# The start of a two-block transformer layer: relative-position masks as signs on ScalarE, the first pass's low parts all on VectorE

## The chip, the cores and the metric

The kernel runs on one core of one Trainium2 chip. The metric is the device time of one execution in microseconds (us), the median of three runs. Engines: TensorE (PE), VectorE (DVE), ScalarE (ACT), GpSimd (POOL) and SyncE (SP), which issues all DMAs here.

## The reference

One sequence of 256 tokens of width 2048 goes through two blocks. Only the head of the first one matters here:

```
mod = silu(c) @ ada_w + ada_b                  # six vectors of 2048: shift, scale, gate, twice
h   = rms_norm(x) * (1 + sc_a) + sh_a
proj = h @ w_in                                # 2048 x 3968 here, latents, rope keys and differential q, k, v
bias = rel_bias[t5_bucket(key_pos - query_pos)]   # 256 x 256 for each of 8 heads
s1, s2 = q1 @ k1 * scale + bias, q2 @ k2 * scale + bias
a = softmax(s1) - lam * softmax(s2)
lam = exp(sum(lq1*lk1)) - exp(sum(lq2*lk2)) + lambda_init
```

Everything is float32. Behind this come the attention of both kinds, an output projection, a convolved gated feed-forward, and a second block with windowed, selected and compressed attention. The change leaves all of that alone.

## The kernel before

**Products.** A float32 product is made as three of a rounded type: each weight half (128 x 1024, 512 KB) is loaded into one of 8 slots of `raw`; ScalarE copies it rounded into `w_hi` (`hi`, L863 to L870), and the difference `raw - w_hi` goes to `w_lo` (`lo`, L1179 on VectorE or L1693 on GpSimd). Both have 4 slots. `product` (L509) issues three matmuls of 128x128 by 128x256 for a weight tile: L514, L515, L516. `hi(h)` waits until TensorE has done with half h - 4. Which engine makes a low part is fixed by the set `POOL_HALVES` (L126): in the first pass the odd halves are GpSimd's, in the second every other one too.

**The passes.** The input projection runs in two passes of 31 units (output tiles), each over 8 of the 16 tiles of the model's width; one unit is one weight half, 24 matmuls. The first pass (`U_IN`) needs the modulation of tiles 0 to 7 of x, the second (`U_IN_B`) of tiles 8 to 15.

**The modulation vectors.** `ada_w` comes in 192 loads of 512 KB, called ada here. VectorE scales each by an element of `silu(c)` and adds it up in `ada_acc` (`ada`, L1187 to L1200). The first 32, ada 0 to 31, make shift and scale of the width's first half, the next 32 those of the second. TensorE then sums over partitions (`mod_sum`, L538 to L547: 16 matmuls of one column for a pair of vectors, f32), VectorE adds the bias (`mod_out`, L1202), and `modulate` (L1230) makes h with ScalarE's `h_high` (L892): x times scale and 1/rms, rounded, and the low part, tile by tile.

**The loads.** SP issues them in one fixed order (`load_order`, L163): ada 0 to 27, weights 0 and 1, ada 28 to 31, weights 2 and 3, then weights and ada 32 to 63 spread evenly. Load n waits until what lies in slot n - 8 is used: for an ada, VectorE's step; for a weight, its low part (`slot_free`, L475). The inputs stand ahead: positions, 0.6 MB of parameters, 0.9 MB of constants; the 2 MB of x stand behind the first eight loads. So load 36, weight 4, waits for the low part of weight 0.

**The bias.** t5_bucket is a step function of the distance. The kernel makes 64 masks of 128 x 256 in bf16, each telling whether key minus query has reached a bucket's start (partitions: 32 starts x 4 groups of keys; one mask for each of 64 key indices), and TensorE sums bucket differences over them, in three bf16 parts: 4 groups of 16 masks, 96 matmuls a group, 48 for each of two query tiles (L665 to L680, 384 in all). ScalarE evicts the eight banks (`bias_ready`, L994 to L1003, four copies each). The banks of the last two groups are shared: bank 6 with the square sums of x, bank 7 with the sums for lambda, so the order in which these stand is an order of banks.

The masks come about like this: ScalarE adds the key's position to `start` for eight masks at a time (`distances`, L970 to L977, 8 activations of 128x256 a block) into one of two buffers, GpSimd compares the block with zero (L1690) and frees the buffer. GpSimd makes blocks 0 to 4 and VectorE blocks 5, 6 and 7 by one comparison each (`last_masks`, L1360), between its first ada.

**Order on each engine up to the first pass.** ScalarE: distances 0 and 1, Sin for the rope tables, distances 2, the squares of x (`squares`, L883, 16 of them into 4 slots), distances 3 and 4, Exp for lambda, root of the mean square, a wait for all of GpSimd's masks, eight evictions, `hi(0)`, `hi(1)`, `h_high`, `hi(2)`, `hi(3)`. TensorE: sum for lambda (behind the product on VectorE at L1396), square sums (L552), bias groups 0, 3, 1, 2, `mod_sum(0)`, `mod_sum(1)`, units. VectorE: positions, bias differences (`delta`), ten steps on 128x256 for cosine and sine (L1379 to L1394), the lambda product, ada 0 to 31 with the masks, after ada 24 the mean of the squares and lambda (L1406 to L1409), after ada 28 the reciprocal; then `mod_out(0)`, `mod_out(1)`, `modulate`, the low parts of weights 0 and 2, and in turns low parts and ada (L1418 to L1422).

```python
            def slot_free(n):
                if n >= RAW_SLOTS:
                    what, i = LOADS[n - RAW_SLOTS]
                    if what == "w":
                        sp.wait_ge(*lo_done(i))
                    else:
                        sp.wait_ge(ada_used, i + 1)
```

## Time and profile before

| | before |
|---|---|
| median of 3 runs | 1955.62 us (1954.48 to 1956.82) |
| the profiled execution | 1954.82 us, of which its span is 1953.0 us |
| mean granted TensorE clock | 0.957 of full |
| PE busy | 1775.6 us, 91% of the span |
| DVE busy | 1253.0 us, 64% |
| ACT busy | 870.9 us, 45% |
| POOL busy | 274.2 us, 14% |
| HBM read | 372.85 MB |

The span runs from the first to the last instruction of the profiled execution; the rest of its time lies around it. Busy time is time in which an engine has an instruction in work; a share over the whole span mixes stages with different limits, so the rows below are taken by stage. Matmuls overlap each other by the time that one needs to drain, so a single one's duration (0.28 us at full clock) is longer than the step from one to the next. A row of the timeline merges equal neighbours: start, time from the first's start to the last's end, engine, line, operation, output and inputs, shapes, count, and in brackets the idle time before it with what ended it.

### The profile page before, as it was taken

The numbers are of one execution on the slowest core, as the hardware profiler recorded it, in microseconds if no ns is written. First come the engines' busy times: TensorE is split into PE (matmuls) and PEld (weight loads), VectorE is DVE, ScalarE is ACT, GpSimd is POOL, SyncE is SP. The second block draws the span as 40 slices with busy tenths as digits, with TensorE's granted clock in tenths as the row PEclk, the third lists the DMA queues.
The fourth block names the chain that finished last, engine by engine and source line by source line (L and its number), as shares of the span: only waits on it lengthen the run. The fifth ranks groups of instructions, "written<-read, shape, count | busy, mean of one in ns | idle before, by whom it ended". The sixth has DMA issues, their size and how long they took to land.

```text
span 1953.0 us, 33440 instructions
## 1 busy us (share of the span) xinstructions
PE 1775.6 (91%) x13960; PEld 1706.7 (87%) x13960; DVE 1253.0 (64%) x1749; ACT 870.9 (45%) x1424; POOL 274.2 (14%) x131
## 2 busy tenths in 40 slices
PE   1399997879998999999999999999699999988997
PEld 1399996778987999999999999999599999866797
DVE  8669698655567766767757756655644446556544
ACT  4444434453445544534535445434444443465442
POOL 7544341001441000000000000000200000152000
PEclk9699998998988999999999999999899999998999
DMA  8499677633973666656656655544155544431041
GB/s 303 162 373 375 229 273 262 202 117 135 337 286 116 224 206 211 232 193 219 230 184 227 223 188 184 184 163 161 54 173 184 183 177 160 162 108 65 33 173 55
DMA packets 102822, 377.13 MB, mean 193 GB/s; under 512 B 11536, under 2 KB 11664, under 8 KB 102544
## 3 DMA queue, kind: packets, MB, share of 16 engines
...
q8 instruction: 111, 1.82, 0.4%
q14 instruction: 39, 0.32, 0.0%
HBM read 372.85 MB, written 2.10 MB: 192 GB/s over the span
## 4 chain that ended last, share of the span: by engine, by line
issue 45%; PE 36%; DVE 13%; POOL 3%; ACT 2%; DMA 1%; SPq 0%; ACTq 0%; DVEq 0%; POOLq 0%
PE ps L514 9%; PE ps L515 9%; PE ps L516 9%; DVE ada_acc L1199 4%; POOL masks L1690 2%; DVE probs L1310 1%; PE ps L596 1%; DVE stats L1284 1%; PE ps L545 1%; DVE w_lo L1184 1%; POOL probs L1684 1%; PE ps L552 1%; PE ps L630 1%; PE ps L615 1%; ACT w_hi L869 1%
## 5 line engine op out<-in xcount | busy, mean ns | idle before, releaser
L514 PE MATMUL ps<-h_hi,w_hi 128*128 128x256 f32 x3264 | 944.0, 289 | 28.2 <-DVE h_lo L1251 8.4
L515 PE MATMUL ps<-h_lo,w_hi 128*128 128x256 f32 x3264 | 930.7, 285 | 0.0
L516 PE MATMUL ps<-h_hi,w_lo 128*128 128x256 f32 x3264 | 930.2, 285 | 0.0
L1184 DVE TENSOR_TENSOR w_lo<-raw,w_hi 128x1024 fp32r<-128x1024 f32 x448 | 552.0, 1233 | 387.7 <-ACT w_hi L869 385.7
L869 ACT ACTIVATE w_hi<-raw 128x1024 fp32r<-128x1024 f32 x512 | 538.8, 1057 | 428.8 <-PE ps L516 408.7
L514 PEld LDWEIGHTS ps<-h_hi,w_hi 128*128 128x128 f32 x3264 | 633.0, 194 | 34.9 <-issue 14.1
L515 PEld LDWEIGHTS ps<-h_lo,w_hi 128*128 128x128 f32 x3264 | 633.9, 194 | 1.1
L516 PEld LDWEIGHTS ps<-h_hi,w_lo 128*128 128x128 f32 x3264 | 633.6, 194 | 0.0
L1199 DVE SCALAR_TENSOR_TENSOR ada_acc<-raw,c_act,ada_acc 128x1024 f32<-128x1024 f32 x180 | 257.7, 1461 | 0.4 <-DMA raw<-in_ada 0.3
L1696 POOL TENSOR_TENSOR w_lo<-raw,w_hi 128x1024 fp32r<-128x1024 f32 x64 | 172.0, 2695 | 426.9 <-ACT w_hi L869 426.9
L514 PE MATMUL ps<-g_hi,w_hi 128*128 128x256 f32 x704 | 200.2, 284 | 3.7 <-DVE g_lo L1528 3.7
L515 PE MATMUL ps<-g_lo,w_hi 128*128 128x256 f32 x704 | 199.8, 284 | 0.0
L516 PE MATMUL ps<-g_hi,w_lo 128*128 128x256 f32 x704 | 199.5, 283 | 0.0
L1684 POOL TENSOR_TENSOR probs<-y,rstd 128x256 f32<-128x256 f32 x32 | 25.1, 803 | 814.5 <-DVE rstd L1228 809.5
L514 PEld LDWEIGHTS ps<-g_hi,w_hi 128*128 128x128 f32 x704 | 134.6, 191 | 4.2 <-DVE g_lo L1528 3.9
L516 PEld LDWEIGHTS ps<-g_hi,w_lo 128*128 128x128 f32 x704 | 132.9, 189 | 0.0
L515 PEld LDWEIGHTS ps<-g_lo,w_hi 128*128 128x128 f32 x704 | 132.5, 188 | 0.3
L1074 ACT ACTIVATE conv<-ps,params 128x256 f32<-128x256 f32 x88 | 49.8, 566 | 152.1 <-PE ps L516 152.1
L1520 DVE SCALAR_TENSOR_TENSOR conv<-ps,params,conv 128x255 f32<-128x255 f32 x88 | 42.5, 482 | 94.3 <-ACT conv L1074 94.3
L917 ACT ACTIVATE probs<-ps,stats 128x128 f32<-128x128 f32 (+1 forms) x112 | 48.7, 439 | 108.0 <-DVE stats L1288 76.5
L874 ACT ACTIVATE proj<-ps 128x256 f32<-128x256 f32 x79 | 30.6, 387 | 130.1 <-PE ps L516 130.1
L552 PE MATMUL ps<-probsT,mean_mat 128*128 128x256 f32 x204 | 62.6, 428 | 16.9 <-ACT probsT L881 16.6
...
## 6 DMA issues: line engine op xcount, KB each, us to landing
raw<-in_weights SPq DMA_DIRECT2D x512, 512.0 KB, 3.6
raw<-in_ada SPq DMA_DIRECT2D x192, 512.0 KB, 4.9
...
```

The lines of the kernel that those rows point to most:

```text
L514: nc.tensor.matmul(out, wh, hi[:, k, :], start=start, stop=False)
L515: nc.tensor.matmul(out, wh, lo[:, k, :], start=False, stop=False)
L516: last = nc.tensor.matmul(out, wl, hi[:, k, :], start=False, stop=stop)
L552: nc.tensor.matmul(ps[:, OUT + NORM[stage] % 2, 0:S], mean_mat[:, :], squares_in(slot), start=first, stop=last).then_inc(sq_used, 1)
L869: nc.scalar.activation(w_hi[:, h % W_SLOTS, :], raw[:, raw_slot("w", h), :], ACT.Copy).then_inc(hi_split, 1)
L917: last = nc.scalar.activation(probs[:, s, off:off + w], ps[:, SCORE + i % 2, off:off + w], ACT.Exp, bias=stats[:, s, 2 + qt:3 + qt], scale ...
L1074: nc.scalar.activation(conv[:, j, :], ps[:, BANK[u], 0:S], ACT.Identity, bias=params[:, col + b:col + b + 1], scale=params[:, col + w1:col ...
L1184: V.tensor_tensor(w_lo[:, h % W_SLOTS, :], raw[:, raw_slot("w", h), :], w_hi[:, h % W_SLOTS, :].bitcast(F32), ALU.subtract).then_inc(lo_dv ...
L1199: V.scalar_tensor_tensor(out=out, in0=part, scalar=c_act[:, k:k + 1], in1=out, op0=ALU.mult, op1=ALU.add).then_inc(ada_used, 1)
L1520: V.scalar_tensor_tensor(out=conv[:, j, 1:S], in0=ps[:, BANK[u], 0:S - 1], scalar=params[:, w0:w0 + 1], in1=conv[:, j, 1:S], op0=ALU.mult, ...
L1684: nc.gpsimd.tensor_tensor(probs[:, at % 2, 0:S], src(k), rstd[:, n % 2, :], ALU.mult).then_inc(scaled, 1)
L1696: nc.gpsimd.tensor_tensor(w_lo[:, h % W_SLOTS, :], raw[:, raw_slot("w", h), :], w_hi[:, h % W_SLOTS, :].bitcast(F32), ALU.subtract).then_i ...
```

## The change

The masks become signs: ScalarE makes all 64 in one activation each, `Sign(start + key position)`, straight into `masks`, four groups of 16 (`signs`). The starts are shifted by a half, so that no distance gives zero; with -1 and 1 in place of 0 and 1 the differences are halved and the last bucket's value is added for the constant part (`tab_last`, two more small steps on VectorE). Distances, their buffers, `neg_pos_k`, GpSimd's and VectorE's comparisons and their semaphores go. TensorE takes the groups in the order 0, 1, 2, 3, the sums for lambda ahead of them and Exp's wait ahead of group 3; the square sums of x come behind all groups, once six evictions are done. ScalarE: signs, Sin, Exp, six evictions, squares, two evictions, root, `hi(0)`, `hi(1)`. The low parts of the first pass are all VectorE's, those of weights 0 and 1 right behind ada 31 and ahead of `mod_out(0)`, those of 2 and 3 behind `modulate`. GpSimd does nothing between its first memsets and the low parts of the second pass. The diff's core:

```diff
-POOL_HALVES = set(range(1, N_IN, 2)) | set(range(N_IN + 1, 2 * N_IN, 2)) | set(range(H_O, H_FF, 2)) | set(
+POOL_HALVES = set(range(N_IN + 1, 2 * N_IN, 2)) | set(range(H_O, H_FF, 2)) | set(
     range(H_CMP + 2, H_OUT2 + 4))
...
-        BIAS_GROUPS = [0, 3, 1, 2]
-        POOL_MASKS = 5
...
             nc.tensor.matmul(ps[:, OUT + 1, 0:2], mean_mat[0:64, :], lam[0:64, 0:2], start=True,
                              stop=True).then_inc(lam_sum, 1)
-            mean_square("x0", KT)
-
-            pe.wait_ge(bias_delta, 1)
-            pe.wait_ge(lam_exp, 1)
-            pe.wait_ge(mean_ready, 1)
-            for i in BIAS_GROUPS:
-                if i == 3:
-                    pe.wait_ge(last_mask, 2)
-                elif i == 2:
-                    pe.wait_ge(last_mask, 3)
-                    pe.wait_ge(bias_mask, POOL_MASKS)
-                else:
-                    pe.wait_ge(bias_mask, 2 * i + 2)
-                for qt in range(0, 2):
+
+            def bias_sums(i):
+
+                pe.wait_ge(bias_mask, i + 1)
+                for qt in range(2):
                     for k in range(16):
                         for part in range(3):
-                            last = nc.tensor.matmul(
-                                ps[:, ds(4 * qt + i, 1), 32 * k:32 * k + 32].rearrange("p a n -> p (a n)"),
-                                masks[:, 16 * i + k, ds(P * qt, P)],
-                                delta3[:, part, :], start=part == 0, stop=part == 2)
+                            last = nc.tensor.matmul(ps[:, 4 * qt + i, 32 * k:32 * k + 32],
+                                                    masks[:, 16 * i + k, P * qt:P * qt + P], delta3[:, part, :],
+                                                    start=part == 0, stop=part == 2)
                     last.then_inc(bias_summed, 1)
+
+            pe.wait_ge(bias_delta, 1)
+            for i in range(3):
+                bias_sums(i)
+            pe.wait_ge(lam_exp, 1)
+            bias_sums(3)
+            pe.wait_ge(bias_ready, 6)
+            mean_square("x0", KT)
             pe.wait_ge(bias_ready, 8)
             mod_sum(0)
...
-            def distances(b):
-
-                if b >= 2:
-                    act.wait_ge(bias_mask, b - 1)
-                for k in range(8):
-                    last = nc.scalar.activation(distance[b % 2][:, k, :], start, ACT.Identity,
-                                                bias=pos_k[:, 8 * b + k:8 * b + k + 1])
-                last.then_inc(distance_ready, 1)
-
-            act.wait_ge(start_ready, 1)
-            distances(0)
-            distances(1)
-
-            act.wait_ge(angle_ready, 1)
-            nc.scalar.activation(cs1[:, :, :], cs1[:, :, :], ACT.Sin).then_inc(cs_ready, 1)
-            distances(2)
-            act.wait_ge(inputs_loaded[4], 16)
-            squares("x0", KT, lambda k: x[:, k, :])
-            distances(3)
-            distances(4)
-            act.wait_ge(lam_sum, 1)
-            nc.scalar.activation(lam[:, 2:4], ps[:, OUT + 1, 0:2], ACT.Exp).then_inc(lam_exp, 1)
-            root("x0")
-            act.wait_ge(bias_mask, POOL_MASKS)
-            for n in range(8):
+            def signs(i):
+
+                for k in range(16 * i, 16 * i + 16):
+                    last = nc.scalar.activation(masks[:, k, :], start, ACT.Sign, bias=pos_k[:, k:k + 1])
+                last.then_inc(bias_mask, 1)
+
+            def bias_out(n):
+
                 act.wait_ge(bias_summed, n + 1)
-                b = 4 * (n % 2) + BIAS_GROUPS[n // 2]
+                b = 4 * (n % 2) + n // 2
                 kk = 16 * (b % 4)
                 for grp in range(4):
                     last = nc.scalar.activation(
@@ -1001,6 +977,21 @@
                         ps[:, b, :].rearrange("p (k g h) -> p k g h", g=4, h=HEADS)[:, :, grp, :],
                         ACT.Copy, scale=1.0 / DIFF_SCALE)
                 last.then_inc(bias_ready, 1)
+
+            act.wait_ge(start_ready, 1)
+            for i in range(4):
+                signs(i)
+            act.wait_ge(angle_ready, 1)
+            nc.scalar.activation(cs1[:, :, :], cs1[:, :, :], ACT.Sin).then_inc(cs_ready, 1)
+            act.wait_ge(lam_sum, 1)
+            nc.scalar.activation(lam[:, 2:4], ps[:, OUT + 1, 0:2], ACT.Exp).then_inc(lam_exp, 1)
+            for n in range(6):
+                bias_out(n)
+            act.wait_ge(inputs_loaded[4], 16)
+            squares("x0", KT, lambda k: x[:, k, :])
+            for n in (6, 7):
+                bias_out(n)
+            root("x0")
             hi(0)
...
-            chain.link(V.tensor_scalar(neg_pos_k[:, :], pos_k[:, :], -1.0, None, ALU.mult))
             dve.wait_ge(inputs_loaded[3], 16)
 
             V.tensor_scalar(start, pos, con("start"), -1.0, ALU.add, ALU.mult).then_inc(start_ready, 1)
-
-            def last_masks(b):
-                dve.wait_ge(start_ready, 1)
-                V.tensor_tensor(masks[:, 8 * b:8 * b + 8, :], start.unsqueeze(1).broadcast_to([P, 8, S]),
-                                neg_pos_k[:, 8 * b:8 * b + 8].unsqueeze(2).broadcast_to([P, 8, S]), ALU.is_ge
-                                ).then_inc(last_mask, 1)
 
             dve.wait_ge(inputs_loaded[0], 16)
             dve.wait_ge(zeros_ready, 2)
             chain.link(V.scalar_tensor_tensor(out=delta[:, 0, :], in0=par("tab_prev"), scalar=con("prev_sign"),
                                               in1=par("tab_next"), op0=ALU.mult, op1=ALU.add))
+            chain.link(V.tensor_tensor(delta[:, 0, :], delta[:, 0, :], par("tab_last"), ALU.add))
+            chain.link(V.tensor_scalar(delta[:, 0, :], delta[:, 0, :], 0.5, None, ALU.mult))
...
             for i in range(32):
                 ada(i)
-                if i in (1, 2, 4):
-                    last_masks({1: 6, 2: 7, 4: 5}[i])
-                elif i == 24:
+                if i == 24:
                     mean("x0", KT, D)
                     dve.wait_ge(lam_exp, 1)
                     chain.link(V.tensor_tensor(lam[:, 4:5], lam[:, 3:4], lam[:, 2:3], ALU.subtract))
                     chain.link(V.tensor_scalar(lam[:, 4:5], lam[:, 4:5], -LAMBDA_INIT, None, ALU.add))
                 elif i == 28:
                     invert("x0")
+            lo(H_IN)
+            lo(H_IN + 1)
             mod_out(0)
             mod_out(1)
             modulate("x0", lambda k: scale_cols[:, 0, k:k + 1], SH_A, 0, SLAB)
-            lo(H_IN)
             lo(H_IN + 2)
+            lo(H_IN + 3)
             item = 32
             for j in range(4, N_IN + 2):
                 lo(H_IN + j)
...
-            for b in range(POOL_MASKS):
-                pool.wait_ge(distance_ready, b + 1)
-                nc.gpsimd.tensor_scalar(masks[:, 8 * b:8 * b + 8, :], distance[b % 2], 0.0, None, ALU.is_ge
-                                        ).then_inc(bias_mask, 1)
-
             def lo(h):
 
                 pool.wait_ge(hi_split, h + 1)
                 nc.gpsimd.tensor_tensor(w_lo[:, h % W_SLOTS, :], raw[:, raw_slot("w", h), :],
                                         w_hi[:, h % W_SLOTS, :].bitcast(F32), ALU.subtract).then_inc(lo_pool, 1)
 
-            for h in range(H_IN + 1, H_IN_B, 2):
-                lo(h)
             for h in range(H_IN_B + 1, H_UQ, 2):
...
+    last = np.where(np.arange(P)[:, None] % 32 == 0, nxt[-1:], 0.0)
...
-    put("start", np.tile(starts, 4))
+    put("start", np.tile(starts - 0.5, 4))
```

## Rows read from the trace of the kernel before

**Rows 1.** Stretches of 20 us: busy time of each engine, clock, DMA share and rate.
```profile
core 0: us, PE busy (x) PEld busy (x) DVE busy (x) ACT busy (x) POOL busy (x), PEclk, DMA share, GB/s
...
40.00:60.00 20.00, 0.00 (x0) 0.00 (x0) 18.50 (x17) 0.00 (x0) 20.00 (x1) 0.51 1.00 390
...
100.00:120.00 20.00, 20.00 (x162) 20.00 (x161) 9.85 (x9) 8.13 (x13) 7.80 (x4) 0.95 1.00 391
```

**Rows 2.** Timeline of the start, ScalarE and GpSimd: masks, distances, tables, evictions.
```profile
8.20 6.47 ACT L975 ACTIVATE bias<-probs,pos_k 128x256 f32<-128x256 f32 x16
...
11.57 10.81 POOL L1690 TENSOR_SCALAR masks<-bias 128x2048 bf16<-128x2048 f32 x2 [7.91 <-ACT bias L975]
...
22.56 0.63 ACT L984 ACTIVATE cs<-cs 128x512 f32<-128x512 f32 x1 [7.89 <-DVE cs L1394]
...
26.46 48.66 POOL L1690 TENSOR_SCALAR masks<-bias 128x2048 bf16<-128x2048 f32 x3 [4.08 <-ACT bias L975]
...
63.42 3.30 ACT L975 ACTIVATE bias<-probs,pos_k 128x256 f32<-128x256 f32 x8 [25.91 <-POOL masks L1690]
66.74 1.28 ACT L991 ACT_TABLE_LOAD   x1
68.03 0.17 ACT L991 ACTIVATE lam<-ps 128x2 f32<-128x2 f32 x1
...
75.16 7.39 ACT L999 ACTIVATE bias<-ps 128x128 f32<-128x128 f32 x32 [5.22 <-POOL masks L1690]
```

**Rows 3.** Timeline of PE: bias sums, mod sums, first pass's first product, second unit, next mod sums.
```profile
68.30 9.93 PE L676 MATMUL ps<-delta,masks 128*128 128x32 bf16 x384 [32.71 <-ACT lam L991]
...
82.59 6.99 PE L545 MATMUL ps<-mean_mat,ada_acc 128*128 128x1 f32 x32 [4.37 <-ACT bias L999]
...
97.50 0.58 PE L514 MATMUL ps<-h_hi,w_hi 128*128 128x256 f32 x1 [7.92 <-DVE w_lo L1184]
...
102.38 0.28 PE L514 MATMUL ps<-h_hi,w_hi 128*128 128x256 f32 x1
...
188.77 3.69 PE L545 MATMUL ps<-mean_mat,ada_acc 128*128 128x1 f32 x32
```

**Rows 4.** Timeline of the squares of x on ScalarE and their sums on PE.
```profile
26.29 1.32 ACT L881 ACTIVATE probsT<-x 128x256 f32<-128x256 f32 x4
26.74 8.85 PE L552 MATMUL ps<-probsT,mean_mat 128*128 128x256 f32 x32 [3.46 <-ACT probsT L881]
...
30.45 3.87 ACT L881 ACTIVATE probsT<-x 128x256 f32<-128x256 f32 x9 [0.32 <-PE ps L552]
```

**Rows 5.** Timeline of VectorE at the start: cosine step, ada, mean, reciprocal, second mod_out.
```profile
11.37 4.66 DVE L1387 SCALAR_TENSOR_TENSOR cs<-cs 128x256 f32<-128x256 f32 x3
...
22.65 1.40 DVE L1196 TENSOR_SCALAR ada_acc<-raw,c_act 128x1024 f32<-128x1024 f32 x2
...
34.17 12.03 DVE L1199 SCALAR_TENSOR_TENSOR ada_acc<-raw,c_act,ada_acc 128x1024 f32<-128x1024 f32 x10
...
58.09 0.41 DVE L1222 TENSOR_SCALAR rstd<-ps 128x256 f32<-128x256 f32 x1
...
76.79 1.74 DVE L1228 RECIPROCAL rstd<-rstd 128x256 f32<-128x256 f32 x1
...
89.69 0.17 DVE L1206 TENSOR_TENSOR mod<-ps,params 128x8 f32<-128x8 f32 x1 [2.90 <-PE ps L545]
```

**Rows 6.** VectorE in the first pass: all ada of 140 to 190 us; one low part.
```profile
L1199 DVE SCALAR_TENSOR_TENSOR ada_acc<-raw,c_act,ada_acc 128x1024 f32<-128x1024 f32 x19 | 40.6, 2177 | 0.0
...
109.70 1.23 DVE L1184 TENSOR_TENSOR w_lo<-raw,w_hi 128x1024 fp32r<-128x1024 f32 x1 [3.14 <-ACT w_hi L869]
```

**Rows 7.** Timeline at the second pass's start: its second mod_out; its second unit's first product.
```profile
193.27 0.17 DVE L1206 TENSOR_TENSOR mod<-ps,params 128x8 f32<-128x8 f32 x1
...
201.07 0.28 PE L514 MATMUL ps<-h_hi,w_hi 128*128 128x256 f32 x1
```

**Rows 8.** Timeline of SP's queue: three weight loads, the last waiting for weight 0's low part.
```profile
74.50 23.30 SPq L488 DMA_DIRECT2D raw<-in_weights  x3
```

9 lines of the change are left out of this document (3 added, 6 removed).

## The prediction

> **What bounds the kernel now.** I read the busy share in stretches first. From 100 to 120 us the PE is busy for all 20 us, with the DMA engines full beside it; from 40 to 60 us it does nothing at all, at a granted clock of about half, while GpSimd is busy for all 20 us [rows 1]. So the kernel has a start during which TensorE waits, and a first pass during which it doesn't. The timeline of ScalarE and GpSimd shows what fills the start: GpSimd makes five mask blocks, two in 10.81 us and three in 48.66 us, the last ending at 75.1 us; ScalarE's distances wait 25.9 us for a buffer that GpSimd has not freed; eight evictions of the bias follow [rows 2]. Only then do the mod sums run (6.99 us), and with the modulation of x behind them the first matmul of the pass starts at 97.50 us and its second unit at 102.38 us [rows 3]. From there to the mod sums of the second half at 188.77 us lie 30 units of 24 products in 86.4 us: 2.88 us a unit, 0.12 us a product, which is PE's own step at the full clock, so nothing waits in it [rows 3]. The start is the target; the first pass must keep its pace.
>
> **The new start, along ScalarE.** Each term is a duration of the trace of before. The steps go along one path; VectorE's own start and the loads are held against it further down.
> 1. The signs. 64 activations of 128x256 take the place of 40 distances. Sixteen distances took 6.47 us, 0.404 us each [rows 2], so 64 x 0.404 = 25.9 us from the same start, 8.20: 34.1 us. No row shows Sign. Bounds from the nearest rows: Square from SBUF at the same width, 9 in 3.87 us or 0.43 us each [rows 4], makes it 1.7 us more; below, nothing excludes that a bf16 output is a tenth cheaper, 2.6 us less. I take 0.404, the row with the same input, width and per-partition bias.
> 2. Sin 0.63, one table load 1.28, Exp 0.17 [rows 2]: 36.2 us. The row of the load ends where Exp begins (66.74 + 1.28 against 68.03), so the load costs 1.28 us. The Trainium skill, in "ScalarE: Activation LUTs", section "What ACT_TABLE_LOAD costs", adds a drain of about 1.38 us to it; by that page this path would be 1.4 us longer and the time 1929.8 us instead of 1928.4. The rows show no such gap.
> 3. Bias sums of groups 0 to 2 cost nothing: 96 matmuls each, a quarter of 9.93 us [rows 3], run from 23 us at the latest (the first ada, at 22.65, stands right behind the lambda product that PE waits for [rows 5]), each behind its own 16 signs, the third from 27.6 us, all under the signs and the table load; uncovered they are 2.5 us each. Group 3 waits for Exp, since its bank holds the lambda sums, and ends at 38.7 under the evictions.
> 4. Six of eight evictions: 7.39 us for all 8 [rows 2], 0.92 each, 5.5 us: 41.8 us. This order is forced: the square sums use the bank of group 2's second half.
> 5. The squares. Before, from the first square at 26.29 to the end of their sums at 26.74 + 8.85 = 35.59 us: 9.3 us, the first ones at ScalarE's wait for a slow PE [rows 4]. Again PE comes from idleness, so the same: 51.1 us. Were it warm, 16 squares would take 16 x 0.43 = 6.9 us, 2.4 less. The load of x, issued behind eight loads, had landed by 26.3 us and is no term.
> 6. VectorE. The mean 0.41, two small operations for lambda (one of that size, the modulation's bias, took 0.17; I count 0.4 with their waits), ada 25 to 30 at 12.03 / 10 = 1.20, and the reciprocal 1.74 between them [rows 5]: 9.8 us, so the last ada that the first mod sum wants is done at 60.8 us. Root and evictions 6 and 7 on ScalarE (1.8 + 1.28 + 0.4 from 49.8) are under the four ada ahead of the reciprocal.
> 7. Mod sums 7.0 us, again from idleness [rows 3]: the second mod_out at 67.8 us. It was at 89.69 [rows 5]: 21.9 us earlier.
>
> **The low parts of weights 0 and 1 moved ahead of the modulation.** They take 2 x 1.23 us [rows 6] on VectorE, under the mod sums (ada 31 ends at 62.0, they at 64.5): nothing, and 2.5 us if the sums were warm. What they free is the first unit, which now follows h tile by tile as the second half's does: there 193.27 to 201.07 from the modulation's bias to the second unit [rows 7], 7.8 us, where before it was 102.38 - 89.69 = 12.7 us. 4.9 us more. The second unit then starts at 75.6 us: **26.8 us earlier**. Behind SP's queue the gain is larger still: it waited 23.3 us for slots of the first weights [rows 8], and everything behind is queued in order. Now the stream restarts at 63 us, 13 us ahead of the second unit, where it had 4.5.
>
> **VectorE's start.** Three masks go; two operations of about 0.2 us come into the chain of the bias differences, ahead of everything behind it, and one outside it goes. Its cosine steps beside GpSimd's masks took 4.66 us for three, where the mean over the same 128x256 took 0.41 [rows 5]; alone they would start ada some microseconds sooner. Even if they don't, ada 24 ends at 22.65 + 0.4 + 1.4 + 23 x 1.20 = 52.1 us [rows 5], 1.0 behind the squares. So this is worth 0 to 1 us on the path; I take 0, since the masks of GpSimd beside those steps are gone. The loads: 28 of 0.52 MB and 3.7 MB of inputs and x are 18.4 MB; at the 390 GB/s of the full stretch [rows 1] they have landed at 47 us or soon after, ahead of their use. The cover of all this is the 1.0 us and more by which ScalarE is late; without it, VectorE's 1.20 us an ada is the path.
>
> **The first pass.** All low parts are VectorE's: per unit 1.23 + 1.10 ada. Beside GpSimd an ada took 2.18 us on average; alone 1.20 [rows 5, 6]. 1.23 + 1.32 = 2.55 us, under PE's 2.88: hidden by PE, with 0.33 us a unit to spare. VectorE takes over 15 low parts. Each of them now waits on VectorE's queue for its high part, and the ada behind it with it, whose slot SP wants back; but a high part is ready at 1.5 us after the unit that frees its buffer, PE wants the low part 8.6 us after it (three units), and ada follow in the order in which SP loads them, so no low part waits for a load that lies behind its own. SP's waits on GpSimd's low parts become waits on VectorE's, at the same places. GpSimd's next work, the second pass's low parts, waits for its high parts as before. The second pass and all behind it keep their program and their pace: 0, and nothing there can swallow the gain, since the loads come as much sooner as PE does.
>
> **Sum.** The profiled execution took 1954.82 us, 1.82 us around its span of 1953.0 and 0.8 us under the median of 1955.62. 1954.82 - 26.8 = 1928.0 us; the median would by the same step be 1928.8, and I give the middle, 1928.4 us.
>
> **Rivals.**
> - **Forecast, 0.72:** 1928.4, its own range 1924 to 1932 (cold and warm PE in steps 5 and 7, at most 2.4 and 3.5 less; Sign at 0.43, 1.7 more).
> - **ScalarE's chain is longer, 0.15.** Sign may need another table set: one load ahead of it and one back for Sin, 2 x 1.28 us; and were Sign a quarter dearer than the distance, that would be 6.5 us. For it: ScalarE is the bound, each us counts. Against: Identity, Copy and Square needed no load in the rows. 1931 to 1937. The skill's same page, "Table sets: the hidden batching unit", names relu, copy, identity and abs as in every set, not Sign; no row here bears on Sign.
> - **VectorE bounds the first pass, slower, 0.03.** If the 2.18 us is not GpSimd's doing but the price of an operation with two inputs from SBUF beside full DMA, and the low parts come to share it, a unit costs 2.10 x 2.18 = 4.6 us, 1.7 over PE, 29 times: +49, net +22, 1977 us. Its turning point is 3.8 us a unit, or 1.81 an operation. For it: it is what VectorE's rows show in the pass. Against: ten ada at 1.20 us from 34 to 46 us [rows 5], and a low part in the pass at 1.23 [rows 6]. If ada alone keeps 2.18, 3.6 a unit, the gain is 26.8 - 21 = 6: 1949 us, 0.03. By the skill's "SBUF — State Buffer", section "Who interferes with whom", a VectorE operation with two SBUF inputs and a GpSimd one that reads exclude each other for a whole instruction, the later one waiting. The rows fit it (GpSimd's mask blocks, 5.4 us each in the first two, took 16.2 in the last three, beside ada at 1.20 [rows 2, 5]); by it neither case can come.
> - **Start hidden anyway, 0.02.** The masks never were the end, or the signs run no sooner than GpSimd's masks did: then the mod sums stay where they are and so does the time, 1955. ScalarE's waits of 25.9 and 5.22 us for GpSimd speak against it [rows 2].
> - **More than the sum, 0.05.** Warm PE throughout: 26.8 + 5.9, 1922.
>
> **Numbers.** A measurement of this kernel can tell about 0.2%, 4 us, from no change. Faster by more: 0.95, same 0.02, slower 0.03. The range of 1921 to 1937 takes in the first, the second and the last case: 0.92, of which I leave a tenth for their own tails.
>
> **What would show it.** Right: the signs end near 34 us; first-pass matmul near 70; second unit near 75.6 with 30 units of 2.88 behind; ada at 1.20 in the pass; SP's stream restarting near 63. Wrong: a table load ahead of Sign; PE waiting in the pass for VectorE's low parts or for weights; a mod sum that starts after 65 us. The forecast fails if VectorE is over 2.88 us a unit or ScalarE's chain to Exp is over 40 us.

## The result, and the profile after

The kernel with the change takes 1922.45 us (median, 1922.31 to 1923.67), the one before beside it 1955.57 us (1954.48 to 1956.82): a ratio of 0.9832, 95% interval 0.9815 to 0.9849, 33.1 us faster. The forecast was 1928.4 us, from a gain of 26.8. The profiled execution took 1922.31 us, its span is 1920.5 us, the mean granted clock 0.959 (0.957 before).

The page of the kernel after, the engines' busy time and the groups that the change touches (busy us, mean ns, then the idle time before):

```profile
PE 1774.3 (92%) x13960; PEld 1705.6 (89%) x13960; DVE 1235.6 (64%) x1762; ACT 879.3 (46%) x1448; POOL 175.7 (9%) x111
...
L1175 DVE TENSOR_TENSOR w_lo<-raw,w_hi 128x1024 fp32r<-128x1024 f32 x463 | 570.4, 1233 | 380.5 <-ACT w_hi L862 378.3
...
L1190 DVE SCALAR_TENSOR_TENSOR ada_acc<-raw,c_act,ada_acc 128x1024 f32<-128x1024 f32 x180 | 237.6, 1340 | 2.2 <-DMA raw<-in_ada 2.2
...
L1677 POOL TENSOR_TENSOR w_lo<-raw,w_hi 128x1024 fp32r<-128x1024 f32 x49 | 131.8, 2698 | 507.9 <-ACT w_hi L862 507.9
```

PE's busy time is the one of before within 1.3 us; what went is waiting. VectorE makes the odd low parts too and is busy for 17 us less, of which its three masks are 6.8; GpSimd is busy for 98 less.

The timeline of the kernel after, from its start to the second unit of the first pass (start, us, engine, line, what, and the wait ahead of it); it answers to [rows 2 to 5] and [rows 8]:

```profile
8.82 25.64 ACT L966 ACTIVATE masks<-probs,pos_k 128x256 bf16<-128x256 f32 x64
...
12.40 1.34 DVE L1373 SCALAR_TENSOR_TENSOR cs<-cs 128x256 f32<-128x256 f32 x3
...
14.98 1.40 DVE L1187 TENSOR_SCALAR ada_acc<-raw,c_act 128x1024 f32<-128x1024 f32 x2
...
34.36 0.61 ACT L985 ACTIVATE cs<-cs 128x512 f32<-128x512 f32 x1
34.99 1.28 ACT L987 ACT_TABLE_LOAD   x1
36.29 0.17 ACT L987 ACTIVATE lam<-ps 128x2 f32<-128x2 f32 x1
36.36 5.66 ACT L975 ACTIVATE bias<-ps 128x128 f32<-128x128 f32 x24
...
36.51 2.74 PE L662 MATMUL ps<-delta,masks 128*128 128x32 bf16 x96 [5.67 <-ACT lam L987]
...
42.37 8.66 PE L547 MATMUL ps<-probsT,mean_mat 128*128 128x256 f32 x32 [3.12 <-ACT probsT L874]
...
51.06 0.42 DVE L1213 TENSOR_SCALAR rstd<-ps 128x256 f32<-128x256 f32 x1 [3.63 <-PE ps L547]
...
51.78 4.87 DVE L1190 SCALAR_TENSOR_TENSOR ada_acc<-raw,c_act,ada_acc 128x1024 f32<-128x1024 f32 x4
...
56.57 1.74 DVE L1219 RECIPROCAL rstd<-rstd 128x256 f32<-128x256 f32 x1
...
60.76 6.96 PE L540 MATMUL ps<-mean_mat,ada_acc 128*128 128x1 f32 x32 [9.73 <-DVE ada_acc L1190]
61.73 2.35 DVE L1175 TENSOR_TENSOR w_lo<-raw,w_hi 128x1024 fp32r<-128x1024 f32 x2
64.11 0.33 SPq L483 DMA_DIRECT2D raw<-in_ada  x1
...
67.83 0.17 DVE L1197 TENSOR_TENSOR mod<-ps,params 128x8 f32<-128x8 f32 x1 [3.12 <-PE ps L540]
...
69.85 0.55 PE L509 MATMUL ps<-h_hi,w_hi 128*128 128x256 f32 x1 [2.13 <-DVE h_lo L1242]
...
75.80 0.41 PE L509 MATMUL ps<-h_hi,w_hi 128*128 128x256 f32 x1
```

The path reads from the top: 64 signs in one block with no table load ahead of them, Sin, one load, Exp, six evictions, squares and their sums, the mean, six more ada with the reciprocal between them, the mod sums, the second mod_out, h tile by tile. The waits in brackets tell which engine is late: VectorE stood for 3.63 us ahead of the mean, waiting for PE's square sums and so for ScalarE.

A stretch of the first pass after, as in [rows 1]:

```profile
100.00:120.00 20.00, 20.00 (x169) 20.00 (x169) 17.81 (x16) 9.15 (x15) 0.00 (x0) 1.00 0.99 380
```

And VectorE's groups in the first pass (mean ns behind the comma), after, and then before:

```profile
L1190 DVE SCALAR_TENSOR_TENSOR ada_acc<-raw,c_act,ada_acc 128x1024 f32<-128x1024 f32 x30 | 40.2, 1351 | 0.0
L1175 DVE TENSOR_TENSOR w_lo<-raw,w_hi 128x1024 fp32r<-128x1024 f32 x29 | 35.5, 1224 | 11.8 <-ACT w_hi L862 11.8
```

```profile
L1199 DVE SCALAR_TENSOR_TENSOR ada_acc<-raw,c_act,ada_acc 128x1024 f32<-128x1024 f32 x29 | 54.8, 1927 | 0.3 <-DMA raw<-in_ada 0.3
L1184 DVE TENSOR_TENSOR w_lo<-raw,w_hi 128x1024 fp32r<-128x1024 f32 x15 | 18.3, 1217 | 17.1 <-ACT w_hi L869 17.1
```

PE is busy throughout with GpSimd at 0.00. Twice as many low parts cost VectorE only 2.6 us on balance, since an ada came down from 1.93 to 1.35 us on average once GpSimd was quiet. These means hide that an ada has two durations. Of the 29 before, 20 took 1.27 to 1.28 us and nine 3.0 to 3.4, each of these beside a low part on GpSimd that had begun before it. Of the 30 after, 29 took 1.28 us. The last took 3.43, beside GpSimd's first low part of the second pass; it is among these three, with GpSimd's row below:

```profile
156.42 5.82 DVE L1190 SCALAR_TENSOR_TENSOR ada_acc<-raw,c_act,ada_acc 128x1024 f32<-128x1024 f32 x3
...
158.20 2.96 POOL L1677 TENSOR_TENSOR w_lo<-raw,w_hi 128x1024 fp32r<-128x1024 f32 x1 [154.53 <-ACT w_hi L862]
```

**Where the time went.** Six marks of each trace, in us from the start of its span. The mod sums are counted from zero: 0 and 1 stand ahead of the first pass, 2 at its end, 4 ahead of the output projection, 6 ahead of the feed-forward, 7 ahead of the feed-forward's last group. The runs below are in it too, so that each can be read against the others.

| kernel | mod sum 0 | second mod_out | first eviction of the pass | mod sum 2 | mod sum 4 | span |
|---|---|---|---|---|---|---|
| before | 82.59 | 89.69 | 102.58 | 188.77 | 458.91 | 1953.0 |
| after | 60.76 | 67.83 | 76.04 | 162.35 | 429.76 | 1920.5 |
| after_again | 61.26 | 68.32 | 76.10 | 161.85 | 427.36 | 1918.2 |
| e1_signs_only | 63.40 | 70.47 | 82.71 | 168.91 | 434.68 | 1925.9 |
| e2_lows_only | 83.05 | 90.14 | 98.04 | 184.24 | 451.22 | 1945.3 |
| e3_lows_late | 61.13 | 68.20 | 81.38 | 167.57 | 437.95 | 1928.8 |
| e4_more_signs | 68.58 | 75.64 | 83.43 | 169.20 | 438.80 | 1929.4 |
| e5_mean_late | 57.79 | 64.86 | 72.64 | 158.39 | 427.18 | 1918.0 |
| e6_pool_beside | 62.39 | 69.46 | 77.25 | 175.53 | 446.90 | 1937.7 |
| s1_before_shifted | 85.54 | 92.64 | 105.64 | 191.82 | 461.91 | 1955.9 |
| e7_order | 55.85 | 62.92 | 70.70 | 156.56 | 426.11 | 1916.9 |
| e8_order_warm | 56.32 | 61.49 | 69.66 | 155.84 | 426.35 | 1917.2 |
| p1_before_moved | 82.85 | 89.95 | 102.58 | 188.77 | 458.39 | 1949.3 |
| p2_best_h_moved | 55.66 | 61.81 | 69.69 | 154.29 | 422.28 | 1887.2 |

Of the 32.5 us between the spans, 26.5 were gained by the first eviction. The first pass gave 0.1 back (86.3 us from the first eviction to mod sum 2, 86.2 before). From there to mod sum 4 the kernel after is 2.7 us quicker (267.4 against 270.1 us), and behind mod sum 4 it is 3.4 us quicker (1490.7 against 1494.1). The change edits no instruction in either of these last two stretches. So two questions: are my reasons for the 26.5 the right ones, and where do the other six come from?

### The profile page after: what moved, and what is told of

Same layout as the page of the kernel before. It is cut to its first block, busy times and chain, and to the rows that moved or that the text cites. A ratio compares the mean times of both kernels' runs of the same rounds, so it can differ in the third digit from the quotient of the medians.

```text
span 1920.5 us, 33456 instructions
## 1 busy us (share of the span) xinstructions
PE 1774.3 (92%) x13960; PEld 1705.6 (89%) x13960; DVE 1235.6 (64%) x1762; ACT 879.3 (46%) x1448; POOL 175.7 (9%) x111
## 4 chain that ended last, share of the span: by engine, by line
issue 45%; PE 40%; DVE 10%; ACT 3%; POOL 1%; DMA 1%; SPq 0%; ACTq 0%; DVEq 0%; POOLq 0%
PE ps L509 11%; PE ps L510 11%; PE ps L511 11%; DVE ada_acc L1190 3%; DVE probs L1301 1%; PE ps L591 1%; ACT masks L966 1%; DVE stats L1275 1%; PE ps L547 1%; PE ps L540 1%; POOL probs L1670 1%; PE ps L625 1%; PE ps L610 1%; PE ps L574 1%; PE ps L633 1%
## 5 line engine op out<-in xcount | busy, mean ns | idle before, releaser
L1175 DVE TENSOR_TENSOR w_lo<-raw,w_hi 128x1024 fp32r<-128x1024 f32 x463 | 570.4, 1233 | 380.5 <-ACT w_hi L862 378.3
L1190 DVE SCALAR_TENSOR_TENSOR ada_acc<-raw,c_act,ada_acc 128x1024 f32<-128x1024 f32 x180 | 237.6, 1340 | 2.2 <-DMA raw<-in_ada 2.2
L1677 POOL TENSOR_TENSOR w_lo<-raw,w_hi 128x1024 fp32r<-128x1024 f32 x49 | 131.8, 2698 | 507.9 <-ACT w_hi L862 507.9
```

Of the source, the lines that this page charges most:

```text
L1175: V.tensor_tensor(w_lo[:, h % W_SLOTS, :], raw[:, raw_slot("w", h), :], w_hi[:, h % W_SLOTS, :].bitcast(F32), ALU.subtract).then_inc(lo_dv ...
L1190: V.scalar_tensor_tensor(out=out, in0=part, scalar=c_act[:, k:k + 1], in1=out, op0=ALU.mult, op1=ALU.add).then_inc(ada_used, 1)
L1677: nc.gpsimd.tensor_tensor(w_lo[:, h % W_SLOTS, :], raw[:, raw_slot("w", h), :], w_hi[:, h % W_SLOTS, :].bitcast(F32), ALU.subtract).then_i ...
```

## The experiments

### Which part of the change brings what

Three kernels take it apart. e1_signs_only keeps the signs and undoes the low parts:

```diff
-POOL_HALVES = set(range(N_IN + 1, 2 * N_IN, 2)) | ...
+POOL_HALVES = set(range(1, N_IN, 2)) | set(range(N_IN + 1, 2 * N_IN, 2)) | ...
...
-            lo(H_IN)
-            lo(H_IN + 1)
             mod_out(0)
...
+            for h in range(H_IN + 1, H_IN_B, 2):
+                lo(h)
```

> The changed kernel with the low parts of the first pass shared out as before (odd halves on GpSimd, those of weights 0 and 2 on VectorE behind the modulation); masks as signs. The forecast's theory: the second mod_out stays near 68 us as in the changed kernel (the signs carry it), the second unit starts 4.9 us later than in the changed kernel (near 81 us), and nothing else moves: 1927.4 us. Rival, that the 6 us which came beyond the forecast hang on GpSimd's absence from the first pass: 1932 to 1933 us, with those us lost between the first pass's end and the attention's start.

Measured: 1930.82 us (1927.64 to 1932.4), ratio 0.9876, interval 0.9861 to 0.9891. Beside it the kernel before took 1954.54 us: the signs alone bring 23.7 us, and at the first eviction 19.9. That is 3.4 us above what I expected, and 2.5 of these are there by the second mod_out, 70.47 where I had 68 (why, is shown below). The rival looked for lost time between the first pass and the attention; there is none, since from mod sum 2 to 4 this kernel takes 265.8 us against 267.4 in the kernel after.

e2_lows_only is the kernel before with all low parts of the pass on VectorE, those of weights 0 and 1 ahead of `mod_out(0)`, and the masks as they were:

```diff
-POOL_HALVES = set(range(1, N_IN, 2)) | set(range(N_IN + 1, 2 * N_IN, 2)) | ...
+POOL_HALVES = set(range(N_IN + 1, 2 * N_IN, 2)) | ...
...
+            lo(H_IN)
+            lo(H_IN + 1)
             mod_out(0)
...
-            for h in range(H_IN + 1, H_IN_B, 2):
-                lo(h)
```

> The kernel before with the low parts alone changed (all of the first pass on VectorE in the order of the loads, weights 0 and 1 ahead of mod_out); masks as before. The forecast's theory: GpSimd's masks still end near 75 us, mod_out stays at 89.7 us, the second unit starts 4.9 us earlier, near 97.5 us: 1950.7 us. If the excess hangs on GpSimd's absence from the first pass: 1945 us. If the gain of 33 us is this part's and not the signs': under 1930 us.

Measured: 1947.09 us (1945.7 to 1948.25), ratio 0.9962, interval 0.9949 to 0.9975: 7.4 us. By the marks, 4.5 us of it lie ahead of the first eviction (step 4.9 of the forecast) and 3.2 between mod sums 2 and 4, of which more below. I had expected 1950.7 us. Counted from the second mod_out to the first eviction, which leaves out small shifts of the start, it takes 7.9 us against 12.9 before.

e3_lows_late is the kernel after with the low parts of weights 0 and 1 behind `modulate`, still on VectorE:

```diff
-            lo(H_IN)
-            lo(H_IN + 1)
             mod_out(0)
             mod_out(1)
             modulate("x0", lambda k: scale_cols[:, 0, k:k + 1], SH_A, 0, SLAB)
+            lo(H_IN)
+            lo(H_IN + 1)
```

> The changed kernel with the low parts of weights 0 and 1 behind the modulation, still on VectorE. By the forecast's term the second unit starts 4.9 us later: 1927.3 us. If that place is worth nothing (the rival: the first unit is bound by h's tiles either way): 1922.5 us. Against the run with the signs alone it tells who makes the low parts from when: equal to it if only the place counts.

Measured: 1927.55 us (1925.97 to 1930.58), ratio 0.9859, interval 0.9842 to 0.9875; the first eviction 5.3 us later than after, the time 5.1 us. Its timeline has the wait of the kernel before back:

```profile
68.20 0.17 DVE L1197 TENSOR_TENSOR mod<-ps,params 128x8 f32<-128x8 f32 x1 [3.11 <-PE ps L540]
...
74.74 4.62 DVE L1175 TENSOR_TENSOR w_lo<-raw,w_hi 128x1024 fp32r<-128x1024 f32 x4
...
76.01 0.58 PE L509 MATMUL ps<-h_hi,w_hi 128*128 128x256 f32 x1 [7.92 <-DVE w_lo L1175]
```

The first product follows its weight's low part, and that stood behind the whole of `modulate` on VectorE's queue. So the two low parts moved ahead are worth the 5 us that the step said: from the second mod_out to the first eviction it takes 13.2 us here and 8.2 in the kernel after, 5.0 apart as in e2.

Between e1 and e3 lies only which engine makes the odd low parts. The paces of their first passes are alike (86.2 us each), yet e1's mod sum 0 starts 2.3 us later. Its timeline shows why:

```profile
52.34 6.96 DVE L1190 SCALAR_TENSOR_TENSOR ada_acc<-raw,c_act,ada_acc 128x1024 f32<-128x1024 f32 x4
```

```profile
55.82 2.39 POOL L1675 TENSOR_TENSOR w_lo<-raw,w_hi 128x1024 fp32r<-128x1024 f32 x1 [52.15 <-ACT w_hi L862]
```

The same four ada took 4.87 us in the kernel after. GpSimd's low part of weight 1 falls beside the last of them, on the path. The forecast priced only the place of the low parts of weights 0 and 1 on VectorE's queue, not what GpSimd's would have cost here. It also closes the account at the first eviction: e1's 19.9 us and e2's 4.5 make 24.4 of the whole change's 26.5, and the 2.1 that are missing are these 6.96 against 4.87.

### Is it ScalarE's chain that sets the new start?

e4_more_signs adds 16 signs of the same form into a tile that nobody reads yet. The rival is that VectorE or the loads are the end by now:

```diff
             for i in range(4):
                 signs(i)
+            for k in range(16):
+                nc.scalar.activation(h_lo[:, k, :], start, ACT.Sign, bias=pos_k[:, k:k + 1])
```

> The changed kernel with 16 more signs ahead of Sin (outputs used by nobody), 16 x 0.40 = 6.4 us of ScalarE. Theory that ScalarE's chain sets the start: the first mod sum, the first eviction and the end come 6.4 us later, 1928.9 us, with VectorE idle 6.4 us longer before its mean. Rival, that VectorE with the loads sets it: VectorE hides part of it, 1925 us or less.

Measured: 1929.47 us (1927.45 to 1931.9), ratio 0.9872, interval 0.9854 to 0.9891: 7.0 us over the kernel after. In its timeline:

```profile
34.73 6.49 ACT L985 ACTIVATE h_lo<-probs,pos_k 128x256 fp32r<-128x256 f32 x16
...
49.05 9.80 PE L547 MATMUL ps<-probsT,mean_mat 128*128 128x256 f32 x32 [3.03 <-ACT probsT L874]
```

Mod sum 0 moved by 7.8 us: 6.4 for the signs, 0.4 for inputs that landed later, 1.1 for square sums at a slower pace, 0.1 less elsewhere. What is added to ScalarE's chain arrives at mod sum 0 in full and at the end, as the forecast had it; the rival, that VectorE hides part of it, is out.

e5_mean_late asks how far the other side, VectorE, is behind. The mean is moved from behind ada 24 to behind ada 27, and the reciprocal behind the two low parts:

```diff
-                if i == 24:
+                if i == 27:
                     mean("x0", KT, D)
...
-                elif i == 28:
-                    invert("x0")
             lo(H_IN)
             lo(H_IN + 1)
+            invert("x0")
```

> The changed kernel with VectorE's mean of the squares and lambda behind ada 27 instead of 24, and the reciprocal behind the low parts of weights 0 and 1. In the changed kernel VectorE stands idle 3.6 us for the squares and makes the reciprocal (1.74 us) ahead of the last ada. By the theory that ScalarE's chain and VectorE's order bind the start, the first mod sum starts 5.3 us earlier, near 55.4 us: 1917.1 us. Rival: the loads of ada 28 to 31, whose slots come free late, bind then: 3 us or less, 1919.5 us or more.

Measured: 1921.51 us (1919.79 to 1921.87), ratio 0.9829, interval 0.9814 to 0.9843. Mod sum 0 starts 3.0 us sooner, not 5.3; the median against the kernel after differs by less than either's spread. The rival is what came true, the loads take over:

```profile
53.85 5.07 DVE L1190 SCALAR_TENSOR_TENSOR ada_acc<-raw,c_act,ada_acc 128x1024 f32<-128x1024 f32 x4 [2.03 <-DMA raw<-in_ada]
```

VectorE waits 2.03 us for ada 28, which stands behind two weights in the order of the loads, and the stretch from 10 to 50 us is full:

```profile
10.00:50.00 40.00, 19.52 (x416) 17.89 (x417) 37.08 (x45) 38.12 (x107) 0.00 (x0) 0.96 1.02 411
```

So the start has three limits close behind one another: ScalarE's chain, then the loads, then VectorE's ada.

### Would the first pass bear GpSimd beside VectorE?

The rival on the slower side said that an ada costs 2.18 us because of the full DMA and not because of GpSimd. The profile after speaks against it. e6_pool_beside puts GpSimd back to work in the first pass, with 15 subtractions whose operands are ready early and whose result nobody reads, each released by an odd high part:

```diff
+            for h in range(H_IN + 1, H_IN_B, 2):
+                pool.wait_ge(hi_split, h + 1)
...
+                nc.gpsimd.tensor_tensor(cmp_side[:, 0:896], consts[:, 0:896], consts[:, 640:1536], ALU.subtract).then_inc(pool_own, 1)
```

> The changed kernel with 15 subtractions of two SBUF inputs on GpSimd (128x896 each, outputs used by nobody) where GpSimd's low parts stood before, beside VectorE's ada and low parts. If GpSimd's operations are what makes ada cost 2.18 us in the kernel before: ada in the first pass goes from 1.20 back to near 1.9 us on average, VectorE then has 37 + 56 = 93 us of work in the first pass's 86, and the pass ends up to 8 us later: 1926 to 1931 us. If the full stream of loads is what makes it dear: ada stays where it is in the changed kernel, 1922.5 us.

Measured: 1937.67 us (1934.17 to 1940.28), ratio 0.9909, interval 0.9886 to 0.9932; the first pass takes 98.3 us instead of 86.3. From its timeline, VectorE and then GpSimd:

```profile
120.08 3.15 DVE L1176 TENSOR_TENSOR w_lo<-raw,w_hi 128x1024 fp32r<-128x1024 f32 x1
...
124.34 1.21 DVE L1176 TENSOR_TENSOR w_lo<-raw,w_hi 128x1024 fp32r<-128x1024 f32 x1
```

```profile
119.54 2.61 POOL L1685 TENSOR_TENSOR cmp_side<-consts 128x896 f32<-128x896 f32 x1 [4.00 <-ACT w_hi L863]
```

The low part at 120.08 ends 1.1 us after GpSimd's operation does, about what one takes alone: as if it did nothing while GpSimd ran. Means over the pass: ada 1.67 us, low parts 1.71. Of these 56 operations thirteen (six ada, seven low parts) took 3.1 to 3.4 us and all others 1.2 to 1.3. So the price is GpSimd's, by the instruction, and no matter which of VectorE's two operations it meets. The Trainium skill says the same in "SBUF — State Buffer", section "Who interferes with whom": the later of the two waits for the whole of the other. The rows agree: 3.15 us for 1.21 here. GpSimd's mask blocks at 16.2 us in place of 5.4 before [rows 2], with VectorE's ada at full pace beside them, fit the other direction, though no run varies that. The 12 us are more than the 8 at most that I expected, and the reason is plain in the stretch from the first eviction to mod sum 2, first of this kernel and then of the kernel after:

```profile
77.25:175.53 98.28, 88.28 (x720) 86.51 (x719) 98.28 (x62) 42.60 (x63) 39.12 (x16) 1.00 0.89 314
```

```profile
76.04:162.35 86.31, 86.31 (x720) 86.31 (x720) 74.55 (x62) 39.92 (x60) 2.96 (x1) 1.00 0.98 366
```

VectorE (third busy time) works for all of the 98.28 us: with GpSimd beside it, it bounds the pass, where in the kernel after it had 11.8 us to spare. PE waits 7.4 us for low parts, and ScalarE's high parts wait 34.8 us for loads, whose slots VectorE gives back late.

### Do the stretches behind follow by themselves?

One theory for the other six: a start at another time meets the clock or the loads in another phase, so that any shift changes what lies behind. s1_before_shifted is the kernel before with five activations ahead of the distances:

```diff
             act.wait_ge(start_ready, 1)
+            for k in range(5):
+                nc.scalar.activation(h_lo[:, k, :], start, ACT.Identity, bias=pos_k[:, k:k + 1])
             distances(0)
```

> The kernel before with five more activations of 128x256 on ScalarE ahead of the first distances (their outputs are used by nobody), 5 x 0.404 = 2.0 us, which GpSimd's masks wait for. If the time behind the start is a fixed 1850 us, as in the kernel before, everything comes 2.0 us later: 1956.5 us or so against 1954.5. Rival, that the 6 us beyond the forecast lie in how the second pass's loads and TensorE's clock happen to fall against the start: the stretch from the first eviction to the end changes by more than 2 us in either direction, most likely shorter, and the time is at or below that of the kernel before.

Measured: 1957.18 us (1953.17 to 1958.71), ratio 1.0008, interval 0.9998 to 1.0018, 1.5 us over the kernel before beside it, which the interval can't tell from none or from 2. The trace can: the first eviction is 3.06 us later, and from there to the end it takes 1850.3 us, where the kernel before takes 1850.4. A shift of this size goes through unchanged; one of 26 us was not tried. after_again ran the changed kernel once more, beside e7 and e8 below.

> The changed kernel itself, beside the two below on one chip: 1922.5 us within 2, the base for both.

Measured: 1923.57 us (1920.01 to 1927.86), ratio 0.9846, interval 0.9823 to 0.9868. From mod sum 2 to mod sum 4 this profile took 265.5 us, where the first took 267.4: the same program twice, 1.9 us apart. Over the fourteen profiles of the table that stretch lies between 265.5 and 271.4 us, in no order that goes with an edit: e3, which is the kernel after but for the place of two operations, took 270.4, the kernel before 270.1, and e2, which has the old masks, 267.0. Part of the 2.7 us lies at the turn to attention. This is the timeline of 16 transposes there, in the kernel before, in the kernel after, and in the second profile of the kernel after:

```profile
300.95 3.68 PE L570 MATMUL ps<-consts,proj 128*128 128x128 f32 x16 [3.50 <-DVE proj L1433]
```

```profile
272.82 1.97 PE L565 MATMUL ps<-consts,proj 128*128 128x128 f32 x16 [1.27 <-DVE proj L1419]
```

```profile
271.40 3.29 PE L565 MATMUL ps<-consts,proj 128*128 128x128 f32 x16 [3.11 <-DVE proj L1419]
```

3.68 us is half clock (granted 0.67 over 300 to 320 us in the kernel before) and 1.97 full, which makes 1.7 of the 2.7 us. But the same program took 3.29 in its second profile, and of all fourteen only that one profile has 1.97, the others 3.3 to 3.7. So this is how one execution fell, and no gain of the change. The granted clock over the whole stretch from mod sum 2 to 4 goes with its length at the ends: 0.96 in the two shortest (265.5 and 265.8 us), 0.93 in the three longest (270.4 to 271.4). Between the kernels before and after it is 0.94 in both, so it doesn't explain their 2.7 us by itself; I made no run that sets the clock here, and the cause stays open.

### The 3.2 us behind: a tile that moved

Behind mod sum 6 the kernel after gains 3.2 us (2.1 to mod sum 7, 1.1 to the end), and most of it comes evenly, 0.5 us at each group of the feed-forward's down projection, whose instructions are the same: from start to start its products are 120.0 ns apart before and 118.7 after, 1.3 ns less, which is 2.7 us over all 2112. What isn't the same is the place of its operands: the change removes `neg_pos_k` (256 bytes in each partition) and widens `params` by 32, so every tile allocated behind it lies 224 bytes lower, the operands `g_hi` and `g_lo` of that projection among them. They lay at 48 bytes beyond a multiple of 64, and lie at 16 beyond. `h_hi` and `h_lo`, allocated ahead, lie at a multiple of 64 in both. p1_before_moved adds one unused tile of 32 bytes to the kernel before, which brings g to 16 beyond a multiple of 64 and changes not one instruction:

```diff
+        moved = sb("moved", [P, 8])
         probsT = sb("probsT", [P, 2, 2 * S])
```

> The kernel before with an unused tile of 8 floats (32 bytes a partition) behind the key positions, so that everything behind it in SBUF, the feed-forward's g_hi and g_lo among it, moves by 32 bytes; the change moved the same tiles by -224. No instruction changes. In the kernel before a product of the down projection takes 0.1200 us, in the changed kernel 0.1187. If the operands' place decides: 0.1187 here too, the stretch from the sixth mod sum to the last shrinks from 722.0 to 719.8 us, and the time is 3 us below the kernel before, about 1952.5 against 1955.5. Rival, that it hangs on something else of the signs' kernel (instructions, instruction loads): 0.1200 and the same time as before.

Measured: 1951.26 us (1946.66 to 1953.32) against 1953.91, ratio 0.9984, interval 0.9974 to 0.9993. Stretches of 40 us in the down projection: kernel before, kernel after, this kernel.

```profile
700.00:740.00 40.00, 40.00 (x336) 40.00 (x335) 23.27 (x29) 15.22 (x15) 0.00 (x0) 1.00 0.54 185
```

```profile
672.00:712.00 40.00, 40.00 (x339) 40.00 (x339) 23.99 (x30) 15.80 (x15) 0.00 (x0) 1.00 0.59 193
```

```profile
700.00:740.00 40.00, 40.00 (x339) 40.00 (x338) 23.54 (x30) 15.80 (x15) 0.00 (x0) 1.00 0.60 191
```

PE at the full clock, never idle, starts 336 matmuls in 40 us before, 339 after, and 339 in the kernel before with the moved tile. PE's count takes in the two or three that were in work when the stretch began; from start to start the products of the moved kernel are 118.7 ns apart, those of h 120.0 in all three. From mod sum 6 to the end that kernel is 3.2 us shorter than the kernel before, as the kernel after is. The other profiles say the same: this stretch takes 1379.8 to 1379.9 us in the three kernels with g at 48 (before, e2, s1), whatever else they change, and 1376.5 to 1377.1 in the ten with g at 16 and h at 0. Of the six us, these three are shown: they come from where tiles lie and not from the work that the change meant to save. Other tiles move with g in all of these runs, and half a microsecond of the 3.2 lies outside g's products.

### Versions that beat both

e7_order builds on e5 and loads ada 28 to 31 ahead of weights 0 and 1, since e5 waited for them:

```diff
-    out = a(0, 28) + w(0, 2) + a(28, 32) + w(2, 4)
+    out = a(0, 32) + w(0, 4)
```

> The changed kernel with the mean behind ada 27, the reciprocal behind the low parts of weights 0 and 1, and ada 28 to 31 loaded ahead of weights 0 and 1. In the run with the late mean alone VectorE waited 2.03 us for the load of ada 28, which stood behind those two weights. If the loads bind there, the first mod sum starts 2.0 us earlier than 57.8 us and 5.0 us earlier than in the changed kernel: 1917.5 us. Rival: the low parts of weights 0 and 1, now loaded last, come late and hold h's modulation: no better than the late mean alone, 1921 us.

Measured: 1919.41 us (1918.73 to 1921.75), ratio 0.9819, interval 0.9802 to 0.9836. Mod sum 0 came 1.9 us sooner than in e5, as expected, and so did the second mod_out; the time is 1.9 us above the one expected. VectorE is close to being late, though: the low parts wait 0.70 us for a high part, as the weights now land last.

e8_order_warm adds ten matmuls without use ahead of the mod sums, so that these don't run at half clock:

```diff
             pe.wait_ge(bias_ready, 8)
+            for k in range(10):
+                nc.tensor.matmul(ps[:, 5, 0:S], mean_mat[:, :], x[:, k, :], start=True, stop=True)
             mod_sum(0)
```

> The kernel above with ten more f32 matmuls of 128x256 on TensorE behind the last bias eviction and ahead of the mod sums (outputs used by nobody). If TensorE's idleness is what lets its clock fall to half ahead of the mod sums, they take 3.5 us instead of 7.0 and the first unit's products run at full clock: 3.5 us less than the kernel above, 1914 us. Rival: the matmuls end late and hold the mod sums, or the clock falls all the same: no gain.

Measured: 1918.07 us (1914.98 to 1919.11), ratio 0.9807, interval 0.9789 to 0.9826, where I had expected 1914. The mod sums came down as meant, and yet little came of it:

```profile
56.32 4.18 PE L540 MATMUL ps<-mean_mat,ada_acc 128*128 128x1 f32 x32
...
59.48 1.75 DVE L1221 RECIPROCAL rstd<-rstd 128x256 f32<-128x256 f32 x1
...
61.15 0.10 DVE L1199 TENSOR_TENSOR mod<-ps,params 128x8 f32<-128x8 f32 x1
```

4.18 us in place of the kernel after's 6.96, but the first mod_out now waits for VectorE, which is still at the reciprocal. The second mod_out is 1.4 us sooner, and the gain over e7 lies within the spread of both.

p2_best_h_moved takes the other finding further: 16 unused bytes ahead of `h_hi` and 48 behind `h_lo`, so that h lies at 16 beyond a multiple of 64 as well, and g stays there:

```diff
+        moved = sb("moved", [P, 4])
         h_hi = sb("h_hi", [P, KT, S], F32R)
...
+        moved2 = sb("moved2", [P, 12])
         params = sb("params", [P, N_PARAMS])
```

> The kernel with the late mean, the loads in another order and the warm mod sums, with h_hi and h_lo moved by 16 bytes (unused tiles of 16 bytes ahead of them and 48 behind, so that all behind them moves by 64). h's products take 0.1200 us in both kernels, g's 0.1187 in the changed one, where g lies at 16 modulo 64 bytes, while h lies at 0 and g at 48 in the kernel before. If 16 modulo 64 is the good place for the moving operand, h's 3264 x 3 products take 0.0013 us less each, up to 13 us: 1906 us. If the place of h doesn't matter, or the good place is another one: 1918 us.

Measured: 1891.85 us (1889.0 to 1894.1), ratio 0.9683, interval 0.9667 to 0.9698. This is 62 us under the kernel before and 26 us under e8 (24 by the two ratios, since they were measured on different chips), twice what I expected. From the pages of e8 and of this kernel, one group of the h products and one of the g products each:

```profile
L509 PE MATMUL ps<-h_hi,w_hi 128*128 128x256 f32 x3264 | 944.5, 289 | 22.6 <-DVE h_lo L1244 10.7
...
L509 PE MATMUL ps<-g_hi,w_hi 128*128 128x256 f32 x704 | 201.1, 286 | 3.7 <-DVE g_lo L1515 3.7
```

```profile
L511 PE MATMUL ps<-h_hi,w_hi 128*128 128x256 f32 x3264 | 934.4, 286 | 24.5 <-DVE h_lo L1246 12.2
...
L511 PE MATMUL ps<-g_hi,w_hi 128*128 128x256 f32 x704 | 200.7, 285 | 3.7 <-DVE g_lo L1517 3.7
```

And 40 us of the up projection, where h moves, in e8 and in this kernel:

```profile
600.00:640.00 40.00, 40.00 (x336) 40.00 (x335) 30.20 (x39) 20.99 (x28) 0.00 (x0) 1.00 0.67 226
```

```profile
600.00:640.00 40.00, 40.00 (x342) 40.00 (x341) 30.47 (x41) 21.32 (x30) 0.00 (x0) 1.00 0.72 234
```

PE at the full clock and never idle has 342 products in work in place of 336; in the feed-forward's full groups they start every 120.0 ns in e8 and, in four of five such groups, every 116.7 here. The two profiled spans are 30.0 us apart (1917.2 against 1887.2). Added up from start to start, with waits left out, 26.0 of these lie in the 9792 products with h, 2.7 ns each on average over all stages, and 0.8 in those with g; the rest lies outside these products.

## Why the prediction was right, and what it missed

The time lies within the range of 1921 to 1937 us, 6 us under the forecast and 1.6 under the likeliest case's own range of 1924 to 1932. The path to the first pass was right in its mechanism; part of the rest came by terms that I had at nothing. Step by step, up to where the path joins the first pass:

| step | forecast | after |
|---|---|---|
| 1, 64 signs | 25.9 us, from 8.20 to 34.1 | 25.64 us, from 8.82 to 34.46 |
| 2, Exp done | 36.2 | 36.46 |
| 3, group 3 of the bias sums done | 38.7 | 39.25 |
| 4, six evictions | 5.5 us | 5.66 us |
| 5, squares and their sums done | 51.1 | 51.03 |
| 6, last ada that mod sum 0 wants | 60.8 | 60.76 |
| 7, second mod_out | 67.8 | 67.83 |
| second unit | 75.6 | 75.80 |
| gain at the second unit | 26.8 us | 26.6 us |

**Right, by runs.** ScalarE's chain is the path: e4 lengthened it, and the end moved with it. Sign costs what Identity does (0.401 us against 0.404) and asks for no table of its own: the only table load ahead of the block is the one at 0.74 us that the kernel before has as well, and none stands between the signs and Sin. The rival with the longer chain falls by that row. The 4.9 us for the low parts moved ahead: e2 and e3 both gave 5.0 from the second mod_out on. The first pass holds PE's pace with all low parts on VectorE, 86.3 us. In e6, with GpSimd at work, an operation cost 1.67 to 1.71 us, and the pass took 12 us more. That is still below the slower rival's turning point of 1.81, at which the whole gain would be gone; with GpSimd idle such prices don't arise.

**Steps that were right for a softer reason.** The 2.55 us a unit for VectorE in the first pass came out as (40.2 + 35.5) / 30 = 2.52, but partly by luck: the sum had 1.10 ada of 1.20 us in a unit, and the trace has 1.0 of 1.34. The 1.20 that it calls the price alone was read from 34 to 46 us, where GpSimd's mask blocks ran beside the ada [rows 2, 5], so that row couldn't show it. On VectorE's start I took 0. The bound worked out there, ada 24 done at 52.1 us, is 1.0 us behind the squares and so no cover at all; the sentence that calls the 1.0 a cover doesn't follow from it. The cosine steps fell from 4.66 to 1.34 us [rows 5] and ada started 7.7 us sooner, so there is a cover after all, 3.63 us, the wait ahead of the mean; e5, which also moved the reciprocal of 1.74 us, got 3.0 us out of the two. SP's stream restarts at 64.1 us, where I had 63. As to the table load: it ends at 34.99 + 1.28 = 36.27 and Exp starts at 36.29, and the one ahead of the root ends at 52.86 with the root at 52.87. By the rule of "ScalarE: Activation LUTs" in the Trainium skill, section "What ACT_TABLE_LOAD costs", a drain of some 1.4 us lies in between; the trace doesn't agree, here as before.

**The step that failed** is the sentence "The second pass and all behind it keep their program and their pace: 0". The program they keep, the pace they don't. That term should have been 3.2 us, because removing one tile and widening another moved the operands of the down projection and made each of its products 1.3 ns shorter, 2.7 us over 2112 products, with 0.5 elsewhere. p1 shows it with 32 bytes and no other edit. The other 2.7 us, between mod sums 2 and 4, belong to a stretch that differs by 1.9 us from one profile of the same program to the next; 1.7 of them are 16 transposes that only one profile of fourteen met at the full clock, and what decides that is open. The rival "more than the sum" gave 1922 us, and the time came out there, but not for its reason: it asked for a warm PE throughout, and PE ran its squares in 8.66 us and its mod sums in 6.96, about what they took before [rows 3, 4]. That the time lies inside that rival's figure is luck.

One small thing was not priced at all. Once the start no longer waits for masks, GpSimd's low part of weight 1 would have fallen beside an ada on the path, 2.1 us (e1). The change has both parts, so it never shows.
